# Sample attention of a decoder layer: keys copied by two engines, scaling moved behind the values

## The chip, the cores and the metric

One Trainium2 chip, one of its cores. The metric is the device time of one execution in microseconds (us); the median of several executions of a kernel is compared. Below, TensorE is also called PE, VectorE DVE, ScalarE ACT, GpSimd POOL and SyncE SP, as the profile does.

## The reference

One step of a decoder layer in float32 for two groups of requests that share their weights: a prompt (1 request, 256 tokens) and a sample group (8 requests with 4 new tokens each, 1024 past tokens). The layer projects the tokens, runs a sparse attention and a gated linear recurrence side by side, merges them under gates, normalizes, and sends the result through a mixture of 32 experts. The change touches the sparse attention of the sample group. It has three branches whose outputs are weighted by sigmoid gates and added:

```
pc = softmax(qn . ck * scale)                      # compressed blocks, 63 of them
o_cmp = pc @ cv
imp = sum of pc over the heads of a group, per block of 64 rows;  keep the 16 best blocks
ps = softmax(qr . k_selected * scale);  o_slc = ps @ v_selected
pw = softmax(qr . k_window * scale);    o_win = pw @ v_window      # the last 512 rows and the new ones
o = g[0] * o_cmp + g[1] * o_slc + g[2] * o_win
```

`o` for the 32 new tokens, 8 query heads and 2 key heads of width 64 is one input of the merge.

## The kernel before, in words

Each engine has one program of its own, written out by hand and kept in step by semaphores; the order of the instructions in each program is the schedule. The stages come one after the other: projections (to 120 us), compression of the cached keys (to 243 us), the recurrence (to 258 us), the prompt's attention (to 321 us), the sample group's attention (to 400 us), the merge, the router, and the experts (from 485 us to the end). Large buffers in SBUF (`big`, `work`, `gates`, `front_rows`) are used by one stage after another.

Into the attention, 16 gate groups are mixed (`gate_group`, L981 to L988): each is 8 products of 128x128 by 128x288, about 4 us of TensorE, that need only early inputs and a gate load of 1 MB for two groups (`load_gates`, L548). They keep TensorE busy while other engines work on the softmax. Each ends in a bank that is copied out by VectorE (groups 3 to 7, L2124) or ScalarE (the others, L1514), and some groups wait for an earlier copy, since they write to the same bank (`FILL_AFTER`): group 5 waits for the copy of group 4.

Sample attention (TensorE from L1053) runs in two halves `s` of four requests. The 128 rows of a half are 16 tokens times 8 heads. In each half:

1. Small scores: against the compressed keys and against the new tokens (L1061, L1064).
2. Keys: the cached keys are 12 sets of 128x512 (sets 0 to 7 from cached blocks, 8 to 11 from the window; set i belongs to request i % 4 of the half). Each is turned by four transposes (L1087) into bank 4 or 5 in turn, copied to one of 8 slots `kt_stage` (ScalarE, `copy_key`, L1532 to L1536), and used by the score products. After set 3, 7 and 11 is copied, `score` (L482 to L491) computes the 128x512 scores of a part, four products; it is called behind set 4, set 8 and set 11. Set n waits for the copy of set n-2, which frees its bank.
3. Meanwhile VectorE and ScalarE make the softmax over the compressed blocks (L2168 to L2179, exponential L1544). One product with `same_group` (L1094) sums it over heads, behind the last score part. From it VectorE chooses two blocks to leave out (L2184 to L2191).
4. Gate groups 8 and 9 (12 and 13 in the second half) run while VectorE adds the choice to the scores (L2196) and takes maxima (L2203, L2204), ScalarE exponentiates 1056 columns of cached blocks and new tokens and 544 columns of the window (L1552), and VectorE scales all by gate over sum (L2193, L2209, L2210).
5. The scaled probabilities are turned in four parts (L1109 to L1113), copied by ScalarE (L1559 to L1562), and after the fourth copy multiplied with the values, 54 products that all add up in the same 128 columns of bank 7 (L1120, L1130). VectorE copies the sum (L2216), TensorE turns it (L1134), VectorE puts it into `nsaT` (L2220). Gate groups 10 and 11 (14 and 15) stand around the turn.

SP issues nearly all loads in program order, and each load can stand behind a wait: gate load 1 and the states of the recurrence `S0` (L556 to L558), cached block rows of the first half (L499), its four window loads (L573 to L576; they overwrite gate loads 2 and 3, so two wait for gate group 5, and two for gate group 7), gate loads 4 and 5, the block rows of requests 2 and 3 of the second half, and its windows. The rows of requests 0 and 1 of the second half are loaded by POOL behind its stores of the new states (L1684). The loads for the merge and the first expert weights are behind waits on the last gate group and on `snsa_copied`.

## Time and profile before

| | us |
|---|---|
| median of 3 runs | 1424.44 (1423.07 to 1424.95) |
| the profiled execution, its own time | 1426.27 |
| its span, first to last instruction | 1424.6 |
| TensorE busy (matmul) | 1381.8 (97%) |
| VectorE busy | 430.2 (30%) |
| ScalarE busy | 302.7 (21%) |
| GpSimd busy | 93.2 (7%) |
| mean granted TensorE clock | 0.993 |

Busy times are sums over the span. A row of the timeline gives start, duration, engine, source line, operation, output and inputs with their sizes, how many such instructions it merges, and in brackets how long the engine was idle before them and which event ended that. PEld is TensorE's weight load, SPq and POOLq are instructions that issue transfers. The granted clock is a share of 2.4 GHz.

### The profile page before, as it was taken

Reading aid. Unit: us, or ns where it says so; the run is one execution under the profiler, and the core shown is the slowest. Engines: PE = TensorE matmul, PEld = TensorE weight load, DVE = VectorE, ACT = ScalarE, POOL = GpSimd, SP = SyncE. Lnnn points to the kernel's source line nnn. Section 1 sums busy time; section 2 is a strip of 40 time slices with the busy share of each in tenths; the row PEclk is TensorE's granted clock in tenths of the full one; section 3 lists DMA queues with packets and bytes.
Section 4 is the critical chain, followed back from the end, with each engine's and each line's share of the span. In section 5 each row is a group of like instructions: output and inputs, shape, how many; then the busy total and the mean of one; then the engine's idle time right before and its main releaser. Section 6 shows DMA issues by size and latency. Waiting matters only on the chain.

```text
span 1424.6 us, 20546 instructions
## 1 busy us (share of the span) xinstructions
PE 1381.8 (97%) x7829; PEld 658.9 (46%) x7829; DVE 430.2 (30%) x938; ACT 302.7 (21%) x519; POOL 93.2 (7%) x122
## 2 busy tenths in 40 slices
PE   9999999998899999999999999999999999999996
PEld 6667999765674533333333333333333333333332
DVE  0346764852225322112211211121113111221115
ACT  1125431443311211111111111111111111111111
POOL 0032300203000000000000000000000000000000
PEclk9999999999999899999999999999999999999998
DMA  8931341729774799999999999999999999999992
GB/s 290 293 98 56 119 149 50 200 67 284 207 297 183 276 418 424 427 428 428 430 427 428 428 428 430 428 428 428 428 429 428 428 428 429 428 429 429 428 428 118
DMA packets 77474, 476.62 MB, mean 335 GB/s; under 512 B 9491, under 2 KB 37459, under 8 KB 52659
## 3 DMA queue, kind: packets, MB, share of 16 engines
q1 hardware_dynamic: 73184, 464.85, 80.5%
q0 software_dynamic: 2288, 9.51, 2.0%
q10 hardware_dynamic: 1954, 1.63, 0.4%
q8 instruction: 29, 0.48, 0.1%
q14 instruction: 19, 0.15, 0.0%
HBM read 471.54 MB, written 8.59 MB: 337 GB/s over the span
## 4 chain that ended last, share of the span: by engine, by line
PE 81%; DMA 13%; DVE 2%; ACT 2%; SPq 1%; issue 0%; ACTq 0%; DVEq 0%
PE bank L1280 25%; PE bank L1313 13%; DMA big<-in_w_gu 12%; PE bank L1252 4%; PE bank L1231 4%; PE bank L987 3%; PE bank L749 3%; PE bank L733 2%; PE bank L1147 2%; PE bank L804 2%; PE bank L806 2%; PE bank L812 2%; PE bank L1160 2%; PE bank L1224 2%; PE bank L1242 1%; PE bank L1302 1%
## 5 line engine op out<-in xcount | busy, mean ns | idle before, releaser
L1280 PE MATMUL bank<-big,gates 128*64 128x512 f32 x1536 | 338.0, 594 | 5.7 <-DMA big<-in_w_gu 5.1
L1280 PEld LDWEIGHTS bank<-big,gates 128*64 128x64 f32 x1536 | 107.9, 137 | 217.5 <-issue 203.3
L1313 PE MATMUL bank<-big,gates 128*64 128x512 f32 x768 | 170.1, 595 | 0.0
L2353 DVE TENSOR_SCALAR gates<-bank 128x512 f32<-128x512 f32 x32 | 22.1, 691 | 437.1 <-PE bank L1293 437.1
L1619 ACT ACTIVATE gates<-gates 128x512 f32<-128x512 f32 x32 | 20.1, 629 | 454.7 <-DVE gates L2353 454.7
L1313 PEld LDWEIGHTS bank<-big,gates 128*64 128x64 f32 x768 | 53.0, 137 | 114.1 <-issue 114.1
L1693 POOL TENSOR_TENSOR gates<-gates,nsaT 128x192 f32<-128x192 f32 x64 | 31.4, 511 | 994.9 <-PE bank L1323 863.2
L2376 DVE TENSOR_TENSOR work<-work,bank 128x512 f32<-128x512 f32 x128 | 82.0, 681 | 42.6 <-PE bank L1252 42.6
L2372 DVE TENSOR_TENSOR work<-work,bank 128x256 f32<-128x256 f32 x32 | 13.5, 421 | 202.2 <-PE bank L1255 202.2
L1252 PE MATMUL bank<-gates 64*128 64x512 f32 x260 | 73.4, 641 | 0.9 <-ACT gates L1629 0.9
L1627 ACT ACTIVATE gates<-bank 128x512 f32<-128x512 f32 x32 | 19.1, 597 | 258.4 <-PE bank L1255 258.4
L987 PE MATMUL bank<-front_cols,big 128*128 128x288 f32 x256 | 65.0, 410 | 1.6 <-DVE gates L2124 1.6
L1231 PE MATMUL bank<-work,gates 128*64 128x512 f32 x264 | 63.9, 605 | 0.0
L1280 PE MATMUL bank<-front_cols,gates 128*64 128x512 f32 x256 | 57.8, 593 | 2.2 <-DMA front_cols<-in_w_gu 2.2
L1280 PE MATMUL bank<-front_rows,gates 128*64 128x512 f32 x256 | 58.1, 595 | 0.0
L987 PEld LDWEIGHTS bank<-front_cols,big 128*128 128x128 f32 x256 | 47.6, 190 | 15.9 <-issue 3.6
L1619 ACT ACT_TABLE_LOAD x32 | 41.1, 1283 | 1.1 <-issue 0.6
L1280 PEld LDWEIGHTS bank<-front_cols,gates 128*64 128x64 f32 x256 | 18.2, 137 | 39.6 <-issue 34.8
L749 PE MATMUL bank<-big,front_cols 128*128 128x512 f32 (+1 forms) x96 | 36.3, 533 | 0.0
L1231 PEld LDWEIGHTS bank<-work,gates 128*64 128x64 f32 x264 | 16.0, 136 | 43.9 <-issue 43.9
L1224 PE MATMUL bank<-work,gates 32*64 32x512 f32 x132 | 35.4, 613 | 0.0
L1293 PE MATMUL bank<-kv,nsaT 32*64 32x512 f32 x256 | 34.8, 613 | 0.0
(387 smaller groups left out, 1624.7 us busy)
## 6 DMA issues: line engine op xcount, KB each, us to landing
big<-in_w_gu SPq DMA_DIRECT2D x96, 2048.0 KB, 24.8
big<-in_w_dn SPq DMA_DIRECT2D x48, 2048.0 KB, 28.1
front_rows<-in_w_gu SPq DMA_DIRECT2D x16, 2048.0 KB, 24.1
front_cols<-in_w_gu SPq DMA_DIRECT2D x16, 2048.0 KB, 25.6
front_rows<-in_w_dn SPq DMA_DIRECT2D x8, 2048.0 KB, 29.3
front_cols<-in_w_dn SPq DMA_DIRECT2D x8, 2048.0 KB, 30.8
big<-in_w_in SPq DMA_DIRECT2D x5, 2048.0 KB, 8.5
big<-in_cache_cmp_kv SPq DMA_DIRECT2D x64, 128.0 KB, 2.6
```

The source lines that it names most:

```text
L733: last = pe.matmul(bank[:, 0:NT], w[:, k, n * P:(n + 1) * P], xTv[:, k, :], start=(k == 0), stop=(k == KD - 1))
L749: last = pe.matmul(bank[0:m, 0:cols], xTv[:, k, t0:t0 + m], w[:, k, 0:cols], start=(k == 0), stop=(k == KD - 1))
L987: last = pe.matmul(bank[:, 0:NT], wg_slot[f // 2][:, k, f % 2 * P:(f % 2 + 1) * P], xTv[:, k, :], start=(k == 0), stop=(k == KD - 1))
L1224: pe.matmul(psum[0][half * CAP:(half + 1) * CAP, :], pick_rows[0:NS, 2, :], h_rows[0:NS, 2, half * 512:(half + 1) * 512], start=True, stop ...
L1231: last = pe.matmul(psum[0][half * CAP:(half + 1) * CAP, :], pick_rows[:, t, :], h_rows[:, t, half * 512:(half + 1) * 512], start=False, st ...
L1252: last = pe.matmul(psum[bank + half][:, :], pgT[rows, t, :], ye[rows, :], start=True, stop=True)
L1280: last = pe.matmul(psum[2 + n][half * CAP:(half + 1) * CAP, :], xe[:, k % 4, (k // 4) * CAP:(k // 4 + 1) * CAP], ring_gu[slot][:, k % 2, c ...
L1293: last = pe.matmul(psum[2 + n][half * CAP:(half + 1) * CAP, :], own_row[rows, :], bias[rows, half * 512:(half + 1) * 512], start=False, st ...
L1313: last = pe.matmul(psum[5][half * CAP:(half + 1) * CAP, :], act_T[:, k % 4, (k // 4) * CAP:(k // 4 + 1) * CAP], ring_dn[slot][:, k % 4, ha ...
L1619: act.activation(sg, g_lim, ACT.Sigmoid, scale=1.702).then_inc(sg_ready, 1)
L1693: last = pool.tensor_tensor(pg[:, :, half, :], pick_rows, gate[:, :, bass.ds(e, 1)].broadcast_to([P, 3, CAP]), ALU.mult)
L2376: dve.tensor_tensor(y, y, psum[6 + half][:, :], ALU.add).then_inc(y_added, 1)
```

## The change

It has five parts.

- **Key copies.** The even sets go to bank 4 and are copied by ScalarE as before. The odd sets go to bank 5 and are copied by VectorE (`take_key`), counted by a new semaphore `key_taken`. VectorE takes set 1 behind the maximum of the block scores, set 3 and the later ones behind their scaling. Score parts 1 and 2 are called behind set 5 and set 9.
- **Windows.** Set 8 of the first half waits for windows 0 and 1 only, set 10 for all four. So that the count means this, SP waits for the first two before it issues the third.
- **Order.** The product with `same_group` comes before score part 3. The transposes of the probabilities wait for the exponentials themselves (the first two parts for the first, the others for the second). The value products wait for each part's copy as they come to it.
- **Scaling.** The probabilities are no longer scaled. The value products add up in three column ranges of bank 7, one for each branch, and three VectorE operations multiply each with its gate over its sum and add them. The sum is turned into a fourth range.
- **Elsewhere.** The states `S0` are loaded before gate load 1. VectorE copies gate group 4 before the maximum of `prompt_max(3)` and not behind it.

The diff, cut to its core:

```diff
@@ score
-            pe.wait_ge(key_copied, 12 * s + 4 * part_ + 4)
+            pe.wait_ge(key_copied, 6 * s + 2 * part_ + 2)
+            pe.wait_ge(key_taken, 6 * s + 2 * part_ + 2)
@@ sync
             sp.wait_ge(hid_done, 12)
-            load_gates(1)
             for b in range(DB):
                 sp.dma_start(S0[:, b, :, :], ins["state_hgrn"][0, b].rearrange("h k v -> k h v")).then_inc(S0_loaded, 16)
+            load_gates(1)
...
                     sp.wait_ge(fill_done, 6 + b4)
+                if b4 == 2:
+                    sp.wait_ge(win_loaded, 32)
                 load_window(0, b4, win_loaded)
@@ tensor
                     if n >= 2:
-                        pe.wait_ge(key_copied, n - 1)
+                        pe.wait_ge((key_copied, key_taken)[n % 2], n // 2)
...
                     if n == 8:
+                        pe.wait_ge(win_loaded, 32)
+                    if n == 10:
                         pe.wait_ge(win_loaded, 64)
...
-                    if i in (4, 8):
+                    if i in (5, 9):
                         score(pe, s, i // 4 - 1)
+                pe.wait_ge(cc_step, 4 * s + 3)
+
+                pe.matmul(psum[0][:, 256:256 + NCS], C("same_group"), s_rows[:, 1600:1600 + NCS], start=True, stop=True).then_inc(cc_step, 1)
                 score(pe, s, 2)
-                pe.wait_ge(cc_step, 4 * s + 3)
-
-                pe.matmul(psum[0][:, 256:256 + NCS], C("same_group"), s_rows[:, 1600:1600 + NCS], start=True, stop=True).then_inc(cc_step, 1)
                 gate_group(8 + 4 * s)
                 gate_group(9 + 4 * s)
 
-                pe.wait_ge(prob_ready, 3 * (s + 1))
                 for q in range(4):
                     n = 4 * s + q
+                    if q in (0, 2):
+                        pe.wait_ge(exp_done, 2 * s + 1 + q // 2)
...
-                pe.wait_ge(st_copied, 4 * (s + 1))
-                out = psum[7][:, 0:P]
                 if s:
-                    pe.wait_ge(snsa_copied, 2)
-                for n in range(2):
-                    pe.matmul(out, s_T[0:NS, 3, n * P:(n + 1) * P], kv[0:NS, 2, (3 + 2 * n) * GD:(4 + 2 * n) * GD],
-                              start=(n == 0), stop=False, skip_group_check=True)
+                    pe.wait_ge(so_copied, 1)
                 for j in range(13):
+                    if j % 4 == 0:
+                        pe.wait_ge(st_copied, 4 * s + j // 4 + 1)
+                    branch = 0 if j < 8 else 1 if j < 12 else 2
...
-                        last = pe.matmul(out[own, :], p, keys, start=False, stop=(j == 12), skip_group_check=True)
+                        last = pe.matmul(psum[7][own, branch * P:(branch + 1) * P], p, keys, start=(j == 0), stop=(j == 12),
+                                         skip_group_check=True)
+                for n in range(2):
+                    last = pe.matmul(psum[7][:, n * P:(n + 1) * P], s_T[0:NS, 3, n * P:(n + 1) * P],
+                                     kv[0:NS, 2, (3 + 2 * n) * GD:(4 + 2 * n) * GD], start=False, stop=True, skip_group_check=True)
                 last.then_inc(spv_done, 1)
@@ scalar
-                act.activation(kt_stage[n % 8], psum[4 + n % 2][:, :], ACT.Copy).then_inc(key_copied, 1)
+                act.activation(kt_stage[n % 8], psum[4][:, :], ACT.Copy).then_inc(key_copied, 1)
...
-                for n in range(3):
+                for n in range(0, 4, 2):
                     copy_key(12 * s + n)
...
-                for n in range(3, 12):
+                for n in range(4, 12, 2):
                     copy_key(12 * s + n)
@@ vector
+                if it == 3:
+                    take_gates(4)
                 dve.wait_ge(ps_step, 4 * (it + 1))
...
             prompt_max(3)
-            take_gates(4)
...
+            def take_key(n):
+
+                dve.wait_ge(key_turned, n + 1)
+                if n >= 8:
+                    dve.wait_ge(scores_done, (n - 8) // 4 + 1)
+                dve.tensor_copy(kt_stage[n % 8], psum[5][:, :]).then_inc(key_taken, 1)
...
                 dve.tensor_scalar(stat[:, 3, 0:1], stat[:, 3, 2:3], -SCALE, None, ALU.mult).then_inc(cc_step, 1)
+                take_key(12 * s + 1)
                 dve.wait_ge(cc_step, 4 * s + 2)
                 dve.reciprocal(stat[:, 3, 1:2], stat[:, 3, 1:2]).then_inc(own.next("c_step"), 1)
                 own.wait("c_step", 3 * s + 3)
                 dve.tensor_scalar(cc, cc, stat[:, 3, 1:2], None, ALU.mult).then_inc(cc_step, 1)
+                for n in range(3, 12, 2):
+                    take_key(12 * s + n)
...
-                dve.tensor_scalar(cc, cc, sgate[:, s, 0:1], None, ALU.mult).then_inc(prob_ready, 1)
...
-                dve.tensor_scalar(s_rows[:, 0:1056], s_rows[:, 0:1056], stat[:, 3, 6:7], None, ALU.mult).then_inc(prob_ready, 1)
-                dve.tensor_scalar(s_rows[:, 1056:1600], s_rows[:, 1056:1600], stat[:, 3, 7:8], None, ALU.mult).then_inc(prob_ready, 1)
-                dve.wait_ge(prob_ready, 3 * (s + 1))
-                step(dve.memset(drop[:, 16:17], 0.0))
...
-                dve.tensor_copy(so_rows, psum[7][:, 0:P]).then_inc(so_copied, 1)
+                step(dve.tensor_scalar(so_rows, psum[7][:, 0:P], stat[:, 3, 6:7], None, ALU.mult))
+                step(dve.scalar_tensor_tensor(out=so_rows, in0=psum[7][:, P:2 * P], scalar=stat[:, 3, 7:8], in1=so_rows, op0=ALU.mult, op1=ALU.add))
+                dve.scalar_tensor_tensor(out=so_rows, in0=psum[7][:, 2 * P:3 * P], scalar=sgate[:, s, 0:1], in1=so_rows,
+                                         op0=ALU.mult, op1=ALU.add).then_inc(so_copied, 1)
```

## Rows read from the trace of the kernel before

**Rows 1.** The page, part 4: shares of the chain that ended last.

```profile
PE 81%; DMA 13%; DVE 2%; ACT 2%; SPq 1%; issue 0%; ACTq 0%; DVEq 0%
```

**Rows 2.** Timeline 230 to 280 us: state loads, state product, gate groups 1 and 2.

```profile
243.00 7.63 SPq L558 DMA_DIRECT2D big<-in_state_hgrn  x8
...
256.53 1.95 PE L921 MATMUL bank<-big,gates 128*32 128x128 f32 x64 [1.39 <-DMA big<-in_state_hgrn]
...
266.48 8.01 PE L987 MATMUL bank<-front_cols,big 128*128 128x288 f32 x32
```

**Rows 3.** Timeline 280 to 320 us: gate groups 4 and 5, maximum, turned probabilities.

```profile
288.35 4.15 PE L987 MATMUL bank<-front_cols,big 128*128 128x288 f32 x16
...
292.74 2.29 DVE L2065 TENSOR_REDUCE small<-big 128x8 f32<-128x2048 f32 x1 [2.86 <-ACT big L1489]
...
295.74 4.12 PE L987 MATMUL bank<-front_cols,big 128*128 128x288 f32 x16 [1.65 <-DVE gates L2124]
...
300.33 1.08 ACT L1509 ACTIVATE big<-bank 128x512 f32<-128x512 f32 x2 [1.02 <-PE bank L1008]
```

**Rows 4.** Timeline from 362 us, second half: key sets, first score part, gate groups.

```profile
363.26 1.07 PE L1087 MATMUL bank<-const,big 128*128 128x128 f32 x8
...
363.98 1.08 ACT L1536 ACTIVATE front_rows<-bank 128x512 f32<-128x512 f32 x2 [0.92 <-PE bank L1087]
...
364.63 1.14 PE L1087 MATMUL bank<-const,big 128*128 128x128 f32 x8 [0.30 <-ACT front_rows L1536]
...
366.79 1.06 PE L490 MATMUL bank<-front_rows,work 128*32 128x512 f32 x8 [0.15 <-ACT front_rows L1536]
...
375.43 7.98 PE L987 MATMUL bank<-front_cols,big 128*128 128x288 f32 x32
```

**Rows 5.** Timeline 299 to 348 us, first half: windows, sets, score part 2, probabilities.

```profile
299.88 22.87 SPq L561 DMA_DIRECT2D big<-in_cache_win_kv  x4
...
321.86 1.07 PE L1087 MATMUL bank<-const,big 128*128 128x128 f32 x8
...
331.33 0.63 PE L1087 MATMUL bank<-const,big 128*128 128x128 f32 x4 [2.99 <-DMA big<-in_cache_win_kv]
...
331.88 1.93 PE L490 MATMUL bank<-front_rows,work 128*32 128x512 f32 x8
...
347.63 1.09 PE L1109 MATMUL bank<-const,work 128*128 128x128 f32 x8 [1.48 <-DVE work L2210]
```

**Rows 6.** Busy time by stretch: us; PE, PEld, DVE, ACT, POOL; clock; DMA share, GB/s.

```profile
321.00:328.00 7.00, 6.14 (x52) 4.06 (x52) 1.66 (x8) 4.00 (x9) 2.52 (x4) 1.00 1.01 273
...
331.30:338.10 6.80, 6.08 (x34) 2.97 (x34) 0.00 (x0) 2.45 (x5) 2.72 (x5) 0.75 1.10 352
```

**Rows 7.** Timeline 376 to 396 us, second half: softmax, probabilities, values, gate group 14.

```profile
377.34 1.28 DVE L2196 TENSOR_TENSOR work<-bank,small 128x512 f32<-128x512 f32 x2
...
380.83 1.18 ACT L1552 ACTIVATE work<-work,small 128x1056 f32<-128x1056 f32 x1 [4.95 <-DVE small L2205]
...
384.79 1.09 PE L1109 MATMUL bank<-const,work 128*128 128x128 f32 x8 [1.39 <-DVE work L2210]
...
387.89 0.71 PE L1120 MATMUL bank<-kv,work 32*128 32x128 f32 x4 [0.77 <-ACT work L1562]
...
391.64 4.15 PE L987 MATMUL bank<-front_cols,big 128*128 128x288 f32 x16
```

**Rows 8.** Groups of VectorE by line and shape: busy us, mean ns, idle before.

```profile
L2039 DVE COPY front_rows<-bank 128x512 f32<-128x512 f32 x2 | 1.3, 686 | 1.5 <-PE bank L933 1.5
```

**Rows 9.** Timeline at 347 to 350 us, then landings of L561 and of L499.

```profile
347.85 15.72 SPq L561 DMA_DIRECT2D big<-in_cache_win_kv  x4
...
349.99 0.54 POOL L499 DMA_DIRECT2D big<-in_cache_slc_kv  x1 [0.60 <-issue]
...
DMA to landing us min/median/max: 3.5/5.7/9.5
...
DMA to landing us min/median/max: 2.0/2.8/6.5
```

More of the change, by code:

```diff
@@ L1088, in _ @@
                     last.then_inc(key_turned, 1)
-                    if i in (4, 8):
+                    if i in (5, 9):
                         score(pe, s, i // 4 - 1)
-                score(pe, s, 2)
                 pe.wait_ge(cc_step, 4 * s + 3)
                 pe.matmul(psum[0][:, 256:256 + NCS], C("same_group"), s_rows[:, 1600:1600 + NCS], start=True, stop=True).then_inc(cc_step, 1)
+                score(pe, s, 2)
                 gate_group(8 + 4 * s)
                 gate_group(9 + 4 * s)
-                pe.wait_ge(prob_ready, 3 * (s + 1))
                 for q in range(4):
                     n = 4 * s + q
+                    if q in (0, 2):
+                        pe.wait_ge(exp_done, 2 * s + 1 + q // 2)
                     if n >= 2:
@@ L1133, in _ @@
                 pe.wait_ge(so_copied, s + 1)
-                pe.transpose(psum[7][:, P:2 * P], so_rows, ident).then_inc(spv_done, 1)
+                if s:
+                    pe.wait_ge(snsa_copied, 2)
+                pe.transpose(psum[7][:, 3 * P:4 * P], so_rows, ident).then_inc(spv_done, 1)
                 gate_group(11 + 4 * s)
@@ L2220, in _ @@
                     dve.tensor_copy(nsaT[rows, :, SEQ + 16 * s:SEQ + 16 * (s + 1)].rearrange("p h t -> p t h"),
-                                    psum[7][rows, P:2 * P].rearrange("p (t y) -> p t y", t=16)[:, :, g * HG:(g + 1) * HG]).then_inc(snsa_copied, 1)
+                                    psum[7][rows, 3 * P:4 * P].rearrange("p (t y) -> p t y", t=16)[:, :, g * HG:(g + 1) * HG]).then_inc(snsa_copied, 1)
             dve.wait_ge(snsa_copied, 4)
```

3 lines of the change are left out of this document (2 added, 1 removed).

## The prediction

> **What bounds the kernel now.** I read the page first, its busy times and the chain that ended last: TensorE is 81% of that chain, transfers are 13% [rows 1]. Then I followed the chain in order of time from 240 to 400 us, and the timeline of all engines beside it, because the edits lie there. The reader should see in each view where TensorE stands still, and what it stood still for. In this stretch it runs almost without a break, and each break is small: 1.39 us for the recurrent state [rows 2], 1.65 us for a gate copy [rows 3], a part of a microsecond after every pair of key sets [rows 4], 3 us for cached window keys, with a lower clock after it [rows 5, 6], 1.4 us for the softmax and 0.8 us for turned probabilities, in both halves of the sample attention [rows 7]. Everything behind 400 us (merge product, router, experts) hangs on the last gate group and is ordered as before, so a microsecond won before that should be a microsecond of the total: the expert weights are not asked for until then.
>
> The profiled execution took 1426.27 us, 1.8 above the median of the three runs (1424.44). I sum against the profiled one and take the same difference off the median.
>
> **State loads ahead of gate load 1.** SP issues gate load 1 (1 MB) just before 243.00 and the eight state loads (2 MB) from 243.00 to 250.63, in one queue; TensorE would start on the states at 255.14 and starts at 256.53 [rows 2]. 3 MB take 13.5 us here, 4.5 us a MB; without 1 MB ahead of them the states land that much sooner, and half of it is enough; if only the issue counts, they land 0.4 us sooner. I take the first, since that MB goes through the same queue, so the whole 1.39 us goes. Bounds: 0.4 and 1.39. Gate load 1 is issued 7.6 us later, at about 250.2; its first reader is gate group 2, in the pair that starts at 266.48 [rows 2], 16 us on, longer than the slowest window load took (9.5 [rows 9]): it costs nothing. The page loads of SP behind both keep their place. What is late next on TensorE: nothing up to the gate copy.
>
> **Gate copy 4 earlier on VectorE.** Now it stands behind the maximum (2.29 us from 292.74), and gate group 5 waits for it 1.65 us, to 295.74 [rows 3]. Ahead of the maximum it waits for the end of gate group 4 (288.35 + 4.15 = 292.50), so group 5 starts at 294.1, as soon as TensorE comes to it. The maximum starts 0.3 us later, and with it ScalarE's exponentials, which end at 299.31 (ScalarE idles 1.02 before 300.33); behind them stand the copies of turned probabilities. The first of these goes at 299.6 in place of 300.33 [rows 3]: there TensorE will wait. So 0.7 us arrives, not 1.65; bounds 0 and 1.65.
>
> **Keys copied by two engines, scores later.** ScalarE copies a 128x512 set in 0.60 us (two in 1.08 plus the overlap) [rows 4]; VectorE needs 0.69 for the same shape from a bank [rows 8]. What counts is the time of one bank: 0.72 us from the start of the transposes to the copy (363.26 to 363.98) and 0.65 from there to the next transposes (364.63) [rows 4], 1.37 for two sets with two banks; a second engine alone hardly shortens it. I worked the second half, t=0 at 363.26, with 0.44 us of transposes for a set and 0.99 for a score part: the busy 1.07 (two sets) and 1.06 [rows 4] less the end that the next one overlaps. Sets 0 to 4 start at 0, 0.44, 1.37, 1.90, 2.74. VectorE takes set 3 only after the reciprocal and the scaling of the block scores, which wait for ScalarE's exponential: at 3.45, not 2.62, so set 5 starts at 4.2. That is what the new wait costs, 1 us with the first score part queued behind it on TensorE. Part 1 is 4.64 to 5.63, sets 6 to 9 start at 5.63, 6.07, 7.0, 7.53, part 2 is 7.97 to 8.96, sets 10 and 11 at 8.96 and 9.40, the group product at 9.84, part 3 at 10.87 when VectorE has copied set 11, end 11.86. Now the gate groups start at 375.43, t=12.17 [rows 4]. Won: 0.3 us.
>
> In the first half the same schedule starts at 321.86 and is at set 10 at 330.8. Now the transposes of set 8 wait for all four windows, to 331.33; then follow, at a clock of 0.75 in that stretch, part 2 at 1.93 us in place of 1.06, four sets and part 3, and the gates start at 338.17 (347.63 less the idle 1.48 and two groups of 3.99) [rows 5, 6]. With a wait for two windows at set 8, only sets 10 and 11, the group product and part 3 stand behind the landing: 331.33, 331.77, 332.21, VectorE's copy to 333.2, part 3 to 334.2 at full clock. Won: 4.0 us, the largest term; at half clock it is 1 to 1.5 us less. The landing itself keeps its distance to TensorE: windows 2 and 3 are issued when gate group 7 ends, the issues ending at 322.75 [rows 5]. The new wait of SP for windows 0 and 1, issued 20 us before, costs nothing.
>
> **Softmax and values.** The group product now comes before part 3, so VectorE's choice of blocks (1.5 us) runs from its last key copy and not behind the scores. The add of the choice to the scores, now at t=14.08 (377.34) [rows 7], comes at 12.45. Two scalings go, and the first two transposes need the first exponential only. That one (380.83 + 1.2 now [rows 7]) would end at 380.4, the second at 381.4, the gate groups at 383.1 (375.12 + 7.98): TensorE goes straight on at 383.1 where it now starts at 384.79 [rows 7]. Won in the second half: 1.7 us, 0.3 of it from above. In the first half the gates end at 342.2, the exponentials at 340.6, where the transposes now start at 347.63 [rows 5]: 5.4 us, 4.0 from above. Then the value products wait for the first of four copies and not for all: from transposes to values now 3.10 us (384.79 to 387.89) [rows 7], new about 2.3, since the transposes of part 4 need the copy of part 2. Won: 0.8 in each half. Three operations of 128 columns on VectorE in place of one copy, each below the 0.69 of a 512 column copy [rows 8], so under 2.1 us, stand beside a gate group of 4.15 us [rows 7]; without that cover they would cost up to 1.8. Number and shape of the value products stay.
>
> **Sum.** 1.4 + 0.7 + (5.4 + 0.8) + (1.7 + 0.8) = 10.8 us. The second half's rows are wanted 1.4 + 0.7 + 6.2 = 8.3 us sooner, at 355.0 (363.26 - 8.3). The last POOL load is issued at 349.99 and the second half's windows from 347.85 [rows 9], 2.1 us earlier in the new kernel; with the slowest landing of their kinds (6.5 and 9.5 us [rows 9]) they are there at 354.4 and 355.7: at most 0.7 us is lost, at their medians nothing.
>
> **The clock.** Between 321 and 328 us, transposes and scores with pauses, the granted clock was 1.00 (2.4 GHz); it was 0.75 on average in the stretch after TensorE stood still for 3 us [rows 5, 6]. In my schedule it idles only 0.5 us there, so I price the first half at full clock. The Trainium skill speaks against that (TensorE: Matmul & The Clock Gate, Part 4: PE-mode transpose): transposes don't count as busy for the clock as products do. By that rule the stretch of transposes would end at half clock and about 2 us less would be won; the 1.00 of 321 to 328 speaks against the rule.
>
> **Rivals.** (A) My schedule is too tight: VectorE, in order, holds each odd set behind its small steps, each half loses 1.5 us more, and sets 10 and 11 then come after the landing. For it: the block chain sits amid VectorE's copies. Against: behind set 3 nothing else is queued. Gain 7.8, 1416.6 us. (B) The clock falls at the window wait nonetheless: 2 us lost, gain 8.8, 1415.6. (C) Loads bind: the states come 0.4 and not 1.39 sooner, the second half's rows 2 us late: gain 7.8, 1416.6. For it: the slowest landings above. (D) Slower: without a long product in between, the key stage falls to half clock in both halves. A score part would cost 0.87 more (1.93 against 1.06 [rows 4, 5]) and a set up to 0.44, 7.9 us a half, 15.8 in all, against a gain of 10.8: 5.0 above, 1429.4. It decides once over 10.8 us, two thirds of this, are lost. Against it is the 1.00 of 321 to 328. (E) No change: the experts are paced by transfers and start no earlier, 1424.4. Against: their loads stand behind the last gate group in SP's queue.
>
> **Chances.** Forecast 0.55, A 0.17, B 0.10, C 0.10, E 0.03, D 0.03, and 0.02 for a gain above 14 that I can't name. Predicted: 1424.44 - 10.8 = 1413.6 us. The range adds 3 us below for terms bounded too low (the gate copy at 1.65, no wait before part 3) and reaches above to A and C with 2 us more: 1410.8 to 1418.6. About 0.2% (2.8 us) is what a measurement of this kernel tells from no change: faster 0.94, same 0.03, slower 0.03.
>
> **What would show it.** The state product starts at 255.1 without idle; gate group 5 at 292.7 (294.1 - 1.4); the first half's wait for windows lies before set 10, under 1 us, and the clock stays at 1.00 behind it; no idle before the probability transposes in either half; the last gate group ends near 389. A wait of TensorE on VectorE of 1 us at set 5 should appear. It is wrong if the window wait stays near 3 us, if the clock there is below 0.9, or if the experts' part grows by what is won ahead of it.

## The result, and the profile after

The changed kernel takes 1414.5 us (median of 5, 1412.14 to 1416.59) against 1423.07 us (1421.99 to 1424.95) for the kernel before on the same chip: ratio 0.9935, 95% interval 0.9923 to 0.9948, so 8.6 to 9.3 us faster. Timed again (run 11 below), it took 1411.81 us (1411.14 to 1414.67) against 1422.85: ratio 0.9924 (0.9909 to 0.9938). The forecast was 1413.6 us, 10.8 below the median before. The profiled execution took 1412.14 us, with a span of 1410.5 and a mean granted clock of 0.997; it is 14.13 us below the profiled one of before, and 10.4 of these lie in the stages that the change touches.

The chain that ended last, shares of the changed kernel's span (page, part 4). The rows [rows 1] have 81% for TensorE and 1% for SP's queue. Three points of the span are some 40 us, three times what was won, so the shares say through which engines the chain is followed and not how much the pauses were worth.

```profile
PE 84%; DMA 12%; DVE 2%; ACT 1%; issue 0%; SPq 0%; ACTq 0%
```

Timeline of the changed kernel, 250 to 302 us: the state product, then the copy of gate group 4 and the maximum on VectorE, gate group 5, the first exponential, and the prompt's turned probabilities.

```profile
255.67 1.96 PE L925 MATMUL bank<-big,gates 128*32 128x128 f32 x64
...
291.67 0.46 DVE L2137 COPY gates<-bank 128x288 f32<-128x288 f32 x1 [2.65 <-PE bank L991]
292.04 2.28 DVE L2078 TENSOR_REDUCE small<-big 128x8 f32<-128x2048 f32 x1
...
293.15 4.15 PE L991 MATMUL bank<-front_cols,big 128*128 128x288 f32 x16
...
294.56 0.51 ACT L1511 ACTIVATE big<-big,small 128x256 f32<-128x256 f32 x1 [2.79 <-DVE small L2080]
...
299.14 1.14 PE L1012 MATMUL bank<-const,work 128*128 128x128 f32 x8 [0.93 <-ACT big L1520]
```

No bracket stands behind the state product or gate group 5 any more [rows 2, 3]. The last row shows the pause that takes the second one's place: TensorE waits 0.93 us for ScalarE, which is behind its exponentials.

First half of the sample attention, timeline of the changed kernel from 318 us: set 4, set 5, sets 8 and 9, sets 10 and 11, score part 3.

```profile
322.69 0.66 PE L1093 MATMUL bank<-const,big 128*128 128x128 f32 x4 [0.16 <-ACT work L1547]
...
324.10 0.65 PE L1093 MATMUL bank<-const,big 128*128 128x128 f32 x4 [0.75 <-DVE work L2181]
...
327.02 1.19 PE L1093 MATMUL bank<-const,big 128*128 128x128 f32 x8 [0.25 <-ACT front_rows L1547]
...
329.26 1.06 PE L1093 MATMUL bank<-const,big 128*128 128x128 f32 x8
...
331.20 1.06 PE L492 MATMUL bank<-work 128*32 128x512 f32 x8 [0.71 <-DVE work L2181]
```

No row has a bracket with `in_cache_win_kv`: the 2.99 us of [rows 5] are gone. Score part 3 takes 1.06 us. Busy time by stretch of the same kernel (columns as in [rows 6]):

```profile
319.00:330.30 11.30, 9.84 (x80) 6.22 (x78) 5.01 (x13) 3.68 (x8) 2.96 (x5) 1.00 1.03 313
329.20:332.30 3.10, 2.34 (x20) 1.42 (x19) 1.69 (x8) 0.60 (x1) 1.11 (x2) 1.00 1.10 350
354.00:366.00 12.00, 9.95 (x80) 6.29 (x78) 5.15 (x14) 4.32 (x9) 0.00 (x0) 1.00 0.92 288
```

The clock column, third from the right, is 1.00 in all three, up to and behind the place where the profile before has 0.75 [rows 6], and in the second half.

Second half, timeline from 354 us: first sets, set 5, score part 3, gate groups 12 and 13, the add of the choice, the first exponential, turned probabilities, values, gate group 14 with the branch sums on VectorE beside it.

```profile
355.03 1.07 PE L1093 MATMUL bank<-const,big 128*128 128x128 f32 x8
...
359.16 0.66 PE L1093 MATMUL bank<-const,big 128*128 128x128 f32 x4 [0.75 <-DVE front_rows L2181]
...
366.17 1.07 PE L492 MATMUL bank<-front_rows,work 128*32 128x512 f32 x8 [0.70 <-DVE front_rows L2181]
...
367.16 8.03 PE L991 MATMUL bank<-front_cols,big 128*128 128x288 f32 x32
...
367.47 1.29 DVE L2218 TENSOR_TENSOR work<-bank,small 128x512 f32<-128x512 f32 x2
...
370.98 1.18 ACT L1563 ACTIVATE work<-work,small 128x1056 f32<-128x1056 f32 x1 [3.09 <-DVE small L2227]
...
375.03 0.60 PE L1116 MATMUL bank<-const,work 128*128 128x128 f32 x4
375.23 0.41 ACT L1525 ACTIVATE gates<-bank 128x288 f32<-128x288 f32 x1 [1.96 <-PE bank L991]
...
375.78 1.25 PE L1116 MATMUL bank<-const,work 128*128 128x128 f32 x8 [0.15 <-ACT gates L1525]
...
377.53 2.83 PE L1135 MATMUL bank<-big,work 128*32 128x128 f32 x96
...
381.28 4.15 PE L991 MATMUL bank<-front_cols,big 128*128 128x288 f32 x16
381.46 0.35 DVE L2234 TENSOR_SCALAR work<-bank,small 128x128 f32<-128x128 f32 x1 [7.80 <-PE bank L1138]
```

Compare with [rows 4, 7]. VectorE's add starts 0.31 us behind the start of the gate groups, where it was 1.91 (377.34 against 375.43), and the turned probabilities follow the gate groups without the pause of 1.39.

To compare kernels, the attention is cut at starts on TensorE. "Keys" run from the small scores to the half's first gate group, "softmax" from there to the first probability transpose, "turn" to the first value product. "Half" runs from small scores to the next half's, or to the merge product. All in us, from one profile each:

| kernel | state product to half 1 | keys 1 | softmax 1 | turn 1 | half 1 | keys 2 | softmax 2 | turn 2 | half 2 |
|---|---|---|---|---|---|---|---|---|---|
| before | 64.61 | 17.03 | 9.46 | 3.10 | 41.41 | 12.88 | 9.36 | 3.10 | 37.06 |
| before_again | 66.30 | 15.44 | 9.36 | 3.10 | 39.72 | 12.88 | 9.36 | 3.10 | 37.06 |
| changed | 63.64 | 12.89 | 7.86 | 2.44 | 35.01 | 12.84 | 7.87 | 2.50 | 34.93 |
| after_again | 63.64 | 12.87 | 7.86 | 2.44 | 34.99 | 12.84 | 7.87 | 2.50 | 34.93 |
| windows_alone | 64.62 | 13.28 | 9.40 | 3.10 | 37.59 | 12.88 | 9.37 | 3.10 | 37.07 |
| order_alone | 64.61 | 16.70 | 7.87 | 3.13 | 39.52 | 12.61 | 7.86 | 3.19 | 35.38 |
| values_alone | 64.62 | 16.91 | 9.38 | 2.26 | 40.37 | 12.88 | 9.38 | 2.26 | 36.24 |
| windows_back | 63.64 | 15.04 | 7.87 | 2.44 | 37.16 | 12.85 | 7.86 | 2.50 | 34.94 |
| one_copier | 63.64 | 13.14 | 7.87 | 2.44 | 35.26 | 12.07 | 7.86 | 2.51 | 34.16 |
| set3_first | 63.64 | 13.13 | 7.87 | 2.44 | 35.25 | 12.02 | 7.86 | 2.50 | 34.10 |
| scaling_back | 63.63 | 13.17 | 7.86 | 2.45 | 35.29 | 12.85 | 7.93 | 2.44 | 34.94 |
| states_back | 63.63 | 13.09 | 7.87 | 2.43 | 35.21 | 12.85 | 7.86 | 2.50 | 34.93 |
| one_copier_early_gate | 63.64 | 13.58 | 7.86 | 2.44 | 35.70 | 12.06 | 7.87 | 2.51 | 34.16 |
| order_only | 63.64 | 13.22 | 7.86 | 2.44 | 35.34 | 12.06 | 7.87 | 2.51 | 34.16 |

Except for keys 1, a cell repeats from kernel to kernel to a few hundredths where its code and clock are the same, so a difference of 0.2 us is read safely there, though no median could show it. Keys 1 also hangs on when windows 2 and 3 and gate load 4 land: four profiles with the same code there (changed, after_again, scaling_back, states_back) have 12.87 to 13.17 us. The merge product starts at 399.61 before and at 389.25 after: 10.36 us, made of 0.86 up to the state product, 0.97 from there to the halves, 6.40 in the first and 2.13 in the second.

Of the 6.40, about 1.6 is a clock fall of the profile before (run 2 below).

The other 3.8 us of the profiled difference lie behind the attention. Busy time by stretch of the kernel before, in its router's stage:

```profile
463.00:470.00 7.00, 6.13 (x39) 4.81 (x38) 5.68 (x15) 1.89 (x4) 0.00 (x0) 0.89 0.79 286
470.00:478.00 8.00, 8.00 (x29) 6.73 (x28) 4.01 (x20) 5.33 (x9) 0.00 (x0) 0.50 1.02 383
```

Of the changed kernel, whose router's stage begins 10.4 us sooner:

```profile
453.00:463.00 10.00, 8.86 (x61) 7.25 (x60) 7.49 (x24) 4.72 (x10) 0.00 (x0) 1.00 0.87 339
463.00:470.00 7.00, 6.50 (x32) 3.21 (x30) 4.22 (x20) 3.76 (x7) 0.98 (x2) 1.00 1.01 375
```

In this stage the granted clock was at its lower level, 1.2 GHz, for some 10 us before and never after. From the router's first transpose to the first expert product it is 22.29 us before (463.54 to 485.83) and 18.90 after (453.17 to 472.07). No edit touches it, and the run states_back shows the same fall with the changed kernel's code there. I don't count these 3.4 us as the change's; what stays open is said in the last section. The merge takes 63.93 and 63.92 us, and the experts some 938.8 and 938.4.

### The profile page after: what moved, and what is told of

It is laid out like the page before. It is cut to its first block, busy times and chain, and to the rows that moved or that the text cites. A ratio compares the mean times of both kernels' runs of the same rounds, so it can differ in the third digit from the quotient of the medians.

```text
span 1410.5 us, 20555 instructions
## 1 busy us (share of the span) xinstructions
PE 1376.1 (98%) x7829; PEld 655.0 (46%) x7829; DVE 436.1 (31%) x946; ACT 296.7 (21%) x507; POOL 93.3 (7%) x122
## 4 chain that ended last, share of the span: by engine, by line
PE 84%; DMA 12%; DVE 2%; ACT 1%; issue 0%; SPq 0%; ACTq 0%
PE bank L1291 25%; PE bank L1324 13%; DMA big<-in_w_gu 12%; PE bank L991 4%; PE bank L1263 4%; PE bank L1242 4%; PE bank L753 3%; PE bank L737 2%; PE bank L1158 2%; PE bank L808 2%; PE bank L810 2%; PE bank L816 2%; PE bank L1171 2%; PE bank L1235 2%; PE bank L1253 1%; PE bank L1313 1%
```

## The experiments

Twelve kernels ran, each timed with 5 to 12 executions, and the kernel before beside them.

**1. The windows alone** (`windows_alone`), on the kernel before:

```diff
+                if b4 == 2:
+                    sp.wait_ge(win_loaded, 32)
                 load_window(0, b4, win_loaded)
...
                     if n == 8:
-                        pe.wait_ge(win_loaded, 64)
+                        pe.wait_ge(win_loaded, 32)
+                    if n == 10:
+                        pe.wait_ge(win_loaded, 64)
```

> The kernel before with the window edit alone (set 8 of the first half waits for windows 0 and 1, set 10 for all four). Theory of the prediction: the wait of 2.99 us before set 8 goes and the clock stays up behind it; by hand set 10 starts near 331.3, score part 3 ends near 334.3, the gate groups start near 334.5 in place of 338.17, so 3.6 us less in the first half and about 1419.5 us in all, TensorE's clock 1.00 from 331 to 338. Rival: the wait only moves from set 8 to set 10 with the clock still falling behind it, so 1 us or less is won and the clock stays at 0.75 there; the order of the group product and the second copier are what won the first half.

1418.89 us (1417.82 to 1422.55), ratio 0.9981 (0.9972 to 0.999). Keys 1 took 13.28 us where the profile before has 17.03: 3.7 us, nearly all of the predicted 4.0, and no other cell moved. The ratio is worth 2.7 us only, and the next run gives a reason.

**2. The kernel before, once more** (`before_again`), nothing changed.

> The kernel before itself, for the spans and clocks of its single executions. Theory: the 3.4 us that the changed kernel's profiled execution won behind 400 us (router stage, clock 0.50 from 470 to 478 us before, 1.00 after) are no effect of the change but a clock that falls there in some executions of either kernel; then executions of this kernel differ by up to 3 us and the longer ones have the lower mean clock. Rival: the fall belongs to the kernel before alone; then all its executions have a clock of 0.993 or less and none is short.

1421.99 us (1421.29 to 1422.51), ratio 0.9991 (0.9982 to 0.9999). Its timeline and stretch, at the same wait for windows:

```profile
332.31 0.63 PE L1087 MATMUL bank<-const,big 128*128 128x128 f32 x4 [2.74 <-DMA big<-in_cache_win_kv]
...
331.20:338.00 6.80, 4.75 (x35) 2.46 (x36) 0.00 (x0) 2.60 (x5) 2.65 (x5) 1.00 1.10 355
```

TensorE waits 2.74 us and the clock stays at 1.00; keys 1 takes 15.44 us. The profile that the prediction was made from has 2.99 us and 0.75 [rows 5, 6]. So the window edit is worth 15.44 - 13.28 = 2.2 us in an execution without the fall, and 3.7 in one with it.

This execution had a fall of its own, elsewhere and earlier. Gate group 5 took 5.81 us where the profile before has 4.12 [rows 3], behind the same wait of 1.65:

```profile
295.28 5.81 PE L987 MATMUL bank<-front_cols,big 128*128 128x288 f32 x16 [1.65 <-DVE gates L2124]
```

The mean granted clock from 294 to 301 us was 0.76 there and 1.00 in the profile before. Its first cell in the table is longer by these 1.69 us. From the state product to the merge both profiles of the kernel before take 143.08 us.

**3. The windows undone** (`windows_back`), in the changed kernel:

```diff
                     if n == 8:
-                        pe.wait_ge(win_loaded, 32)
-                    if n == 10:
                         pe.wait_ge(win_loaded, 64)
```

> The changed kernel with set 8 of the first half waiting for all four windows again. Theory: the window edit is the largest term; TensorE stands still before set 8 for 2.5 to 3.5 us, two sets, parts 2 and 3 and the group product lie behind the landing, and if the clock falls there as before, the first half's stretch from the small scores to the gate groups grows from 12.9 to about 16 us and the total by about 3 us, to 1416 where the router stage keeps its clock. Rival: with the new order of scores and copies the stretch grows by 1 us or less.

1415.75 us (1413.15 to 1418.37), ratio 0.9955 (0.9941 to 0.9968). From its timeline and its stretches:

```profile
328.39 1.06 PE L1091 MATMUL bank<-const,big 128*128 128x128 f32 x8 [2.62 <-DMA big<-in_cache_win_kv]
...
331.20:338.00 6.80, 6.09 (x32) 4.20 (x31) 5.28 (x14) 1.89 (x3) 2.96 (x6) 1.00 1.06 340
```

Keys 1 is 15.04 against 12.89: 2.15 us, the same as the first two runs give. The 16 us that were expected took a clock fall for granted; there is none behind this wait of 2.62 us.

**4. One copier** (`one_copier`): ScalarE copies all twelve sets, the score parts stay where the change put them.

```diff
-                act.activation(kt_stage[n % 8], psum[4][:, :], ACT.Copy).then_inc(key_copied, 1)
+                act.activation(kt_stage[n % 8], psum[4 + n % 2][:, :], ACT.Copy).then_inc(key_copied, 1)
...
-                for n in range(3, 12, 2):
-                    take_key(12 * s + n)
```

> The changed kernel with all key copies on ScalarE again, in two banks, score parts at their new places. Theory: the time of one bank (transposes to copy to transposes, 1.37 us for two sets) sets the pace, so the second engine brings within 0.5 us of nothing in each half and the total is within 1 us of the changed kernel. Rival: ScalarE's own copies (0.6 us each, 12 of them) set the pace; then without VectorE each half is 1.2 us or more longer and the total 2.4 us or more above the changed kernel.

1410.98 us (1410.54 to 1411.54), ratio 0.9916 (0.9903 to 0.9929): the second copier wins nothing, and the cells show it as a loss. Its second half:

```profile
357.80 0.65 PE L1091 MATMUL bank<-const,big 128*128 128x128 f32 x4 [0.20 <-ACT front_rows L1545]
...
358.61 0.66 PE L1091 MATMUL bank<-const,big 128*128 128x128 f32 x4 [0.16 <-ACT front_rows L1545]
359.20 1.06 PE L490 MATMUL bank<-front_rows,work 128*32 128x512 f32 x8
...
365.44 1.06 PE L490 MATMUL bank<-front_rows,work 128*32 128x512 f32 x8 [0.57 <-ACT front_rows L1545]
```

From the first transposes of the half (355.09), set 5 starts at 3.52 where the changed kernel has it at 4.13 (359.16 - 355.03), and part 3 at 10.35 where it has 11.14. Keys 2 is 12.07 us, 0.77 less. In the first half nothing is won: TensorE waits 0.71 us there for windows 2 and 3 and 0.31 for gate load 4, and keys 1 is 13.14.

**5. Set 3 copied first** (`set3_first`): two copiers, but VectorE takes set 3 ahead of the reciprocal.

```diff
                 take_key(12 * s + 1)
+                take_key(12 * s + 3)
                 dve.wait_ge(cc_step, 4 * s + 2)
...
-                for n in range(3, 12, 2):
+                for n in range(5, 12, 2):
```

> The changed kernel with VectorE's copy of set 3 moved ahead of the reciprocal and the scaling of the block scores, nothing else. Theory: what makes the changed kernel's second half 0.8 us longer than with one copier is the 0.75 us wait of TensorE for VectorE's copy of set 3 (behind ScalarE's exponential), so set 5 starts 0.75 us sooner, the second half's stretch from the small scores to the gate groups falls from 12.85 to 12.1 us and the total by 0.7; the first half gains little, since gate load 4 lands only there. Rival: the second copier is slow because a VectorE copy takes 0.69 us against ScalarE's 0.60 in each of six sets; then this changes nothing (0.2 us or less).

1411.43 us (1410.77 to 1412.29), ratio 0.9919 (0.9906 to 0.9932). Its second half:

```profile
357.21 1.23 PE L1093 MATMUL bank<-const,big 128*128 128x128 f32 x8 [0.21 <-ACT front_rows L1547]
...
358.38 1.06 PE L492 MATMUL bank<-front_rows,work 128*32 128x512 f32 x8
```

Sets 4 and 5 are one row now, and keys 2 is 12.02 us. The loss was the place of one copy in VectorE's order. Without it two copiers reach 12.02 and one reaches 12.07: a second engine brings 0.05 us.

**6. The scaling put back** (`scaling_back`) ahead of the transposes, with one sum for the branches, the rest as changed.

```diff
+                pe.wait_ge(h_clear, 3 * (s + 1))
                 for q in range(4):
                     n = 4 * s + q
-                    if q in (0, 2):
-                        pe.wait_ge(exp_done, 2 * s + 1 + q // 2)
...
-                        last = pe.matmul(psum[7][own, branch * P:(branch + 1) * P], p, keys, start=(j == 0), stop=(j == 12),
+                        last = pe.matmul(psum[7][own, 0:P], p, keys, start=(j == 0), stop=(j == 12),
...
+                dve.tensor_scalar(cc, cc, sgate[:, s, 0:1], None, ALU.mult).then_inc(h_clear, 1)
...
+                dve.tensor_scalar(s_rows[:, 0:1056], s_rows[:, 0:1056], stat[:, 3, 6:7], None, ALU.mult).then_inc(h_clear, 1)
+                dve.tensor_scalar(s_rows[:, 1056:1600], s_rows[:, 1056:1600], stat[:, 3, 7:8], None, ALU.mult).then_inc(h_clear, 1)
```

The semaphore `h_clear`, which is in the kernel anyway, counts the three scalings of a half.

> The changed kernel with the probabilities scaled before the transposes again (three VectorE operations in each half, transposes wait for them), values added in one range. Theory after reading the trace of the changed kernel: the second exponential ends at 373.3, the gate groups at 375.0, and the scalings take 1.6 us, so they nearly fit beside the gate groups; the move of the group product is what took the 1.4 us wait away, and this costs less than 0.5 us in all. Rival: the scalings are on the path, each half loses their 1.3 us, 2.5 us in all.

1412.61 us (1411.42 to 1415.14), ratio 0.9931 (0.9918 to 0.9944): nothing is lost. From its timeline:

```profile
373.73 0.77 DVE L2231 TENSOR_SCALAR work<-work,small 128x1056 f32<-128x1056 f32 x1
374.42 0.50 DVE L2232 TENSOR_SCALAR work<-work,small 128x544 f32<-128x544 f32 x1
374.97 2.00 PE L1115 MATMUL bank<-const,work 128*128 128x128 f32 x12
```

The scalings end at 374.92, 0.05 us before the transposes start. Softmax 2 is 7.93 us where the changed kernel has 7.87, so TensorE stood still for them 0.06 us at most. It is nearly a tie: the removal would pay as soon as the gate groups were shorter.

**7. The group product alone** (`order_alone`), in the kernel before:

```diff
-                score(pe, s, 2)
                 pe.wait_ge(cc_step, 4 * s + 3)
 
                 pe.matmul(psum[0][:, 256:256 + NCS], C("same_group"), s_rows[:, 1600:1600 + NCS], start=True, stop=True).then_inc(cc_step, 1)
+                score(pe, s, 2)
```

> The kernel before with one edit: the product of the group sums goes ahead of the third part's score products in each half. Nothing else: one copier, the four scalings ahead of the transposes, the old window wait. Theory: the 1.4 to 1.5 us that the probability transposes came earlier in the changed kernel (start of the half's gate products to first transpose 9.36 to 9.46 us before, 7.86 after) is this move alone; so here that stretch is 7.9 to 8.0 us in both halves, the second half is about 35.6 us where it was 37.06, and the whole time is 1.0025 times smaller, about 1419 us (ratio 0.998, some 0.1 lower than that if the move of both halves comes through whole). Rival: the exponential's waits and the scalings are needed too, since here the transposes still wait for all four scalings: then the stretch is over 9 us and the time that of the kernel before (ratio 1.000).

1420.43 us (1418.33 to 1423.07), ratio 0.998 (0.997 to 0.9989). From its timeline:

```profile
373.75 8.03 PE L987 MATMUL bank<-front_cols,big 128*128 128x288 f32 x32
...
381.61 0.60 PE L1109 MATMUL bank<-const,work 128*128 128x128 f32 x4
```

Softmax is 7.87 and 7.86 us, 1.6 and 1.5 us less, with the three scalings by gate and sum still ahead of the transposes. Keys 2 is 0.27 us shorter besides, since the product fills a wait for the last copy. A line moved by one place is worth 1.68 us in the second half.

**8. The value products' wait alone** (`values_alone`), in the kernel before:

```diff
-                pe.wait_ge(st_copied, 4 * (s + 1))
                 out = psum[7][:, 0:P]
...
                 for j in range(13):
+                    if j % 4 == 0:
+                        pe.wait_ge(st_copied, 4 * s + j // 4 + 1)
```

The two products of the compressed branch go behind the others.

> The kernel before with one edit: the value products wait for each part of the turned probabilities by itself, and the two products of the compressed branch come last in the same sum. Theory: first probability transpose to first value product 2.45 us in both halves where it was 3.10, and nothing else: 1.3 us of the whole, ratio 0.999. Rival: the wait only moves behind the first group of value products, so that the first value product is earlier and the last one is not: then the half is as long as before (37.06 us in the second) and the ratio is 1.000.

1420.46 us (1419.44 to 1423.41), ratio 0.998 (0.9971 to 0.9989). Turn is 2.26 us in both halves, 0.84 less, where 0.65 was expected, and the second half is 0.82 us shorter (36.24): the wait doesn't come back behind the first products.

**9. Gate load 1 ahead of the states again** (`states_back`), in the changed kernel:

```diff
+            load_gates(1)
             for b in range(DB):
                 sp.dma_start(S0[:, b, :, :], ins["state_hgrn"][0, b].rearrange("h k v -> k h v")).then_inc(S0_loaded, 16)
-            load_gates(1)
```

> The changed kernel with gate load 1 ahead of the state loads again. Theory: TensorE waits 1.1 to 1.4 us for the states before its state product, and all behind it comes as much later: total 1.2 us above the changed kernel. Rival: something behind (gate load 4, windows, the exponentials of the prompt) takes the gain back before 390 us, so the total differs by less than 0.4 us.

1413.18 us (1412.42 to 1416.99), ratio 0.9928 (0.9915 to 0.9941). The pause is back:

```profile
256.89 1.96 PE L925 MATMUL bank<-big,gates 128*32 128x128 f32 x64 [1.14 <-DMA big<-in_state_hgrn]
```

Its fastest execution took 1412.42 us and that of the changed kernel 1411.14, both at a mean clock of 0.997: 1.3 us, about what the pause says. Its router's stage shows the fall that the profile before has, though nothing there differs from the changed kernel:

```profile
463.00:470.00 7.00, 7.00 (x28) 6.28 (x27) 3.14 (x15) 4.35 (x10) 0.00 (x0) 0.52 1.02 368
```

**10. One copier, and gate load 4 issued ahead of windows 2 and 3** (`one_copier_early_gate`), since run 4's gate groups waited 0.31 us for that load.

```diff
             for b4 in range(4):
+                if b4 == 2:
+                    sp.wait_ge(pv_done, len(ITS))
+                    load_gates(4)
                 if b4 % 2 == 0:
                     sp.wait_ge(fill_done, 6 + b4)
...
-            sp.wait_ge(pv_done, len(ITS))
-            load_gates(4)
```

> The one-copier version with gate load 4 issued ahead of windows 2 and 3 (as soon as the prompt's last values are done, some 4 us sooner than gate group 7 ends). Theory: in the one-copier version the first half's gate groups wait for this load (0.31 us of TensorE, 1.2 of its weight load), though the second half shows that the keys need 12.1 us and the first takes 13.1; so the first half's stretch falls by up to 1 us, to 12.1 or to what windows 2 and 3 allow, and the total to about 1410. Rival: the 1 MB ahead of the windows delays them by 2 us or more, the wait moves to set 10 and the total rises by 1 us.

1416.77 us (1412.33 to 1419.03), ratio 0.9954 (0.9936 to 0.9971). The rival came true:

```profile
329.28 1.06 PE L1092 MATMUL bank<-const,big 128*128 128x128 f32 x8 [1.52 <-DMA big<-in_cache_win_kv]
```

A megabyte put ahead in the same queue makes sets 10 and 11 wait 1.52 us where run 4 waited 0.71. Keys 1 is 13.58 us, 0.44 more. Most of the higher median isn't from there: its executions at 1418.9 to 1419.0 have mean clocks of 0.991 to 0.992, and those at 0.996 took 1412.3 to 1413.9.

**11. The changed kernel, once more** (`after_again`).

> The changed kernel, unaltered. Theory: its time differs between executions by the router's stage alone: with a mean granted clock of 0.996 or more it takes 1412 to 1413.5 us, with 0.994 or less 1414.5 to 1416.6 us, and sample attention's halves are 35.0 and 34.9 us in its profile either way. Rival: something in the changed kernel's attention differs between executions, and a profile shows a half over 35.5 us.

1411.81 us (1411.14 to 1414.67), ratio 0.9924 (0.9909 to 0.9938). The halves are 34.99 and 34.93 us, as before. The five executions at a mean clock of 0.996 or 0.997 took 1411.1 to 1412.5 us, and the one at 0.994 took 1414.67. The first measurement had three of five executions at 0.993 or 0.994 (1414.5 to 1416.6 us). So most of what differs between the two is the clock, and the theory had its levels about 1 us too high.

**12. Order and waits alone** (`order_only`): the changed kernel with runs 4 and 6 together, so without the two parts that brought nothing.

> The changed kernel with both of the things undone that single experiments found to bring nothing: ScalarE copies all key sets, and the four scalings stand ahead of the transposes as before, with one sum for the branches. What is left is order and waits alone: state loads first, gate copy 4 ahead of the maximum, the windows' wait split, the score parts one set later, the group product ahead of the third part, the value products waiting part by part. Theory: the whole gain is in these, and the second half's keys keep the 0.8 us that one copier gave: 1410.5 to 1411.5 us where the clock is 0.996 or more, ratio 0.992, keys of the second half 12.1 us, start of gate products to first transpose 7.9 us in both halves. Rival: the copier and the scaling cover for each other (with ScalarE copying all the sets its exponentials come later, and the scalings behind them then end behind the gate products): the transposes wait 0.5 us or more in a half, and the time is 1412 us or above.

1410.49 us (1410.32 to 1415.24), ratio 0.9915 (0.9899 to 0.9931). All cells are as the theory says, keys 2 at 12.06 us and softmax at 7.86 and 7.87. It has the lowest median, some 1.3 us under the changed kernel's (1411.81), though their intervals overlap. The profiles show 0.44 us of that in the attention: from the state product to the merge it is 133.14 us against 133.58. The rest isn't explained. What binds its first half are two transfers:

```profile
328.44 1.06 PE L1091 MATMUL bank<-const,big 128*128 128x128 f32 x8 [0.59 <-DMA big<-in_cache_win_kv]
...
331.80 1.48 PE L989 MATMUL bank<-front_cols,big 128*128 128x288 f32 x5 [0.49 <-DMA big<-in_w_in]
```

## Why the prediction was right, by its own steps

The sum took 10.8 us off the median and gave 1413.6 us, in a range of 1410.8 to 1418.6; measured were 1414.5 and, once more, 1411.81. The trace has 10.36 us, the first ratio 9.3 and the second 10.8. (Three us below 1413.6 is 1410.6; the lower end in the text is 0.2 off its own rule. And three scalings go, not two: the third, of the compressed branch, stood off the path.)

**States**, predicted 1.4. The pause went whole; the run that brings it back has 1.14 us. The product itself moved by 0.86 only, because the stage ahead of it, which no edit touches, ended 0.5 us later in this execution (255.67 against 255.14). The step was right.

**Gate copy 4**, predicted 0.7, measured 0.97 (64.61 to 63.64). That ScalarE would be late next was right (the pause of 0.93). The term was small because I had the exponentials start 0.3 us later behind the copy; they start 2.92 us behind the end of gate group 4 where it was 2.77, so 0.15 later. No run undoes this edit alone; the 0.97 is read from the two profiles: 1.65 us of waiting gone, and 0.93 in place of 0.25 behind it (299.14 after, 300.98 before).

**First half**, predicted 4.0 + 1.4 + 0.8, measured 4.14 + 1.60 + 0.66. Sets 10 and 11 had no bracket, where 0.5 us of idle was forecast; in five other profiles with this window edit and the new order they wait 0.24 to 1.07 us for the landing, so it still sets the pace there. Runs 1 to 3 correct the reading of the largest term: 2.2 us of it are the wait, and 1.6 (17.03 against 15.44) the clock behind it, which falls in some executions and not in others. I took one profiled execution for all of them, so that this term came out within 0.2 us is partly luck. Less that fall the trace has about 8.8 us and not 10.36. Both profiles of the kernel before lost 1.6 to 1.7 us to a fall ahead of the merge, in two different places, and of its variants windows_alone lost none; how often its executions do, the profiles can't say.

**Second half**, predicted 0.3 + 1.4 + 0.8, measured 0.04 + 1.49 + 0.60. The hand schedule had set 5 at 4.2 us and the row says 4.13. It had part 3 at 10.87 and the row says 11.14: from set 8 on each pair of sets takes a little longer than my 0.44 a set, and that is 0.2 of the missing 0.27. The value products came 0.66 and 0.60 us sooner and not 0.8. Run 8 alone has 0.84. There ScalarE is idle when the transposes start; in the changed kernel it copies a gate group out first (0.41 us at 340.26 and at 375.23), and the second part's transposes wait for that copy too. That VectorE's order costs time at set 5 was right (TensorE waits 0.75 us there, and 1 was forecast), and run 5 shows how to have it back: there the first score part starts at 3.88 us and not at 4.71.

**What each part brought.** Here the prediction was vaguer than it could have been. It gave the softmax term three causes together: the product's place, two scalings fewer, an earlier wait. Run 7 gives all 1.5 us to the first, run 6 nothing to the second. It said that a second engine hardly shortens a bank's round trip, but kept the later score parts and the copier in one term. The second half separates them: 12.88 before, 12.61 with the product moved (run 7), 12.06 with the score parts one set later as well (run 12), 12.84 with the second copier (changed). So the order won 0.8 us and the copier gave it back.

**The branch sums.** Three operations of 0.35 us stand beside a gate group of 4.15, at no cost, in place of one copy of 0.29. I had bounded them by 0.69 each.

**The clock.** The stretch of transposes and score products ran at a granted clock of 1.00 to its end (319 to 330.3, 329.2 to 332.3) in this profile, and no stretch of the sample attention was lower in the eight of runs 3 to 6 and 9 to 12. The rule that I weighed, the Trainium skill, TensorE: Matmul & The Clock Gate, Part 4: PE-mode transpose, that transposes don't count as busy for the clock, would have cost 2 us there; the trace disagrees with it here.

**Rivals.** A: VectorE held set 3 and no other, and the windows had landed when TensorE came to sets 10 and 11. B: the clock stayed at 1.00. C: the pause for the states, 1.14 to 1.39 us, went whole, and no row of the second half was waited for. D: no stretch of the keys fell to half clock. E: the experts start 13.8 us sooner, the 10.4 of the attention and the 3.4 of the router.

## What to carry to other kernels

Look for the product that other engines wait for and put it ahead of the long ones behind it: one line moved one place won 1.5 us and more in each half, where the second copier and the removed scaling together won nothing. Where two banks take turns, the round trip of a bank (transposes, copy, hand-over) sets the pace, and a second copying engine only adds its own order as a new way to wait. Ask of every profiled execution whether its clock falls are in all executions before a gain is priced by them, and undo each part of a many-part change alone: here the copier and the branch sums could be left out, and the kernel without them took 1410.5 us where the changed one took 1411.8, within their noise.

## What the runs showed of the hardware that was not expected

**The same pause with and without a clock fall.** Five profiles have a long wait for windows in the first half. Behind waits of 2.62 and 2.74 us the granted clock stayed at 1.00 in the next stretch; behind 2.99, 3.01 and 3.07 us (the profile before, values_alone, order_alone) it was 0.75. The stretch of order_alone:

```profile
331.20:338.00 6.80, 5.60 (x34) 3.28 (x34) 0.96 (x5) 2.39 (x4) 2.38 (x5) 0.75 1.10 356
```

By these five alone it would look as if 0.3 us more of waiting decided. The wait for gate copy 4 speaks against that: it is 1.65 us in all five profiles of the old order, and behind it the clock fell in one (before_again, 0.76) and stayed at 1.00 in four. So the length of the pause alone doesn't decide, and what does is open. The size is shown: the kernel before takes 17.03 us for keys 1 with the fall and 15.44 without it, and 5.81 us for gate group 5 with it and 4.12 without.

**A clock fall with no long pause.** In the router's stage small transposes and 128x32 products follow one another with short pauses (0.35 us at most on TensorE between 463.5 and 470 us in the profile before), and the clock falls to 0.50. It stays there for some 10 us in four profiles (before, order_alone, states_back, one_copier_early_gate), for some 3.4 us in two (before_again, windows_alone), and doesn't fall in the other eight. The long fall costs 3.4 us in the profile before. The kernels of the changed order showed a fall in 2 of 9 profiles and those of the old order in 4 of 5; whether the change lowers its odds is not settled by so few. If it does, a part of these 3.4 us belongs to it after all. The Trainium skill (TensorE: Matmul & The Clock Gate, Part 1: The HAM clock gate) says that one kernel can show different numbers of slow products at its start from run to run; here the same is seen in the middle of a kernel.
